# The selected-value pages of sample 7 are issued by SyncE in place of GpSimd

## The reference, cut to what matters

```
z = x @ w_in                                   # one projection for all groups
nsa_past = cache_nsa_kv[l, page_table]         # 8 samples x 16 pages of 128 rows, [cmp_k, cmp_v, sel_k, sel_v]
imp = einsum('bqn,ns->bqs', p.sum(axis=2), cover)     # importance of blocks of 64 rows
_, idx = top_k(imp, 16)                        # first block and two local ones always in
kg, vg = ks[bi, idx], vs[bi, idx]
sc = einsum('bqhd,bqjsd->bqhjs', q, kg) * ATTN_SCALE
o_sel = einsum('bqhjs,bqjsd->bqhd', softmax(sc), vg)
...
mix = concat([y_conv, o_nsa, o_moba, y_pool]) @ w_out
x = layer_norm(ALPHA * x + mix);  x = layer_norm(ALPHA * x + square(relu(x @ w_up)) @ w_down)
```

## Time and profile before

| | |
|---|---|
| Runs shown | 795.03, 796.51, 799.62 us |
| Median | 796.51 us |
| The profiled execution | 796.34 us |
| Its span | 794.6 us |
| Mean granted TensorE clock | 0.983 |
| Busy, share of the span | PE 95%, DVE 54%, ACT 35%, POOL 26% |
| selV pages by GpSimd (L1438) | 64 issues of 32 KB |
| selV pages by SyncE (L640) | 64 issues of 32 KB |

### The profile page before, as it was taken

One profiled execution on the slowest core, in us unless ns is written; L12 is line 12 of the kernel. 1 busy time (PEld: TensorE's weight loads), 2 busy tenths in 40 slices (PEclk: granted clock), 3 DMA queues, 4 the chain that ended last, 5 costly groups with the idle time before them and its releaser, 6 DMA issues.

```text
span 794.6 us, 17023 instructions
## 1 busy us (share of the span) xinstructions
PE 752.9 (95%) x6744; PEld 658.2 (83%) x6744; DVE 433.0 (54%) x744; ACT 281.8 (35%) x542; POOL 206.5 (26%) x268
## 2 busy tenths in 40 slices
PE   9999999988887999799999999999999999999992
PEld 8998988764554555369999999999999999999991
DVE  4878994554545543445866656534563255533535
ACT  5232234544535322342444454312431134311124
POOL 0000625012224555100837731000210012100083
PEclk9999999989999999899999999999999999999997
DMA  9656762547789885312252333332323322333102
GB/s 336 178 157 174 211 191 74 212 170 283 277 283 310 243 282 159 126 38 81 71 185 80 84 103 105 108 94 75 99 80 107 105 77 86 106 85 102 54 1 108
DMA packets 62680, 113.26 MB, mean 143 GB/s; under 512 B 16873, under 2 KB 34026, under 8 KB 61930
## 3 DMA queue, kind: packets, MB, share of 16 engines
q1 hardware_dynamic: 56074, 95.40, 38.7%
q0 software_dynamic: 6528, 16.78, 6.3%
HBM read 107.72 MB, written 6.52 MB: 144 GB/s over the span
## 4 chain that ended last, share of the span: by engine, by line
PE 75%; issue 8%; DVE 7%; DMA 3%; ACT 3%; POOLq 3%; POOL 1%; ACTq 0%; DVEq 0%
PE psum L723 58%; PE psum L732 4%; POOLq L1437 2%; DMA moba_lo<-in_moba_pages 1%; DMA moba_hi<-in_moba_pages 1%; PE psum L777 1%; PE psum L840 1%; PE psum L1004 1%; PE psum L808 1%; DVE yc L1579 1%; POOLq L1428 1%; DVE wL L1510 1%; PE psum L854 1%; PE psum L750 1%; PE psum L992 1%
## 5 line engine op out<-in xcount | busy, mean ns | idle before, releaser
L1510 DVE TENSOR_TENSOR wL<-raw,wH 128x1024 fp32r<-128x1024 f32 (+1 forms) x92 | 117.7, 1280 | 94.0 <-ACT wH L1155 94.0
L1155 ACT ACTIVATE wH<-raw 128x1024 fp32r<-128x1024 f32 (+1 forms) x92 | 94.0, 1022 | 120.4 <-PE psum L723 119.9
L723 PE MATMUL psum<-oxH,wH 128*128 128x260 f32 (+1 forms) x512 | 105.0, 286 | 1.5 <-DVE wL L1510 0.9
L723 PE MATMUL psum<-oxH,wL 128*128 128x260 f32 (+1 forms) x512 | 103.9, 284 | 0.0
L723 PE MATMUL psum<-oxL,wH 128*128 128x260 f32 (+1 forms) x512 | 103.4, 283 | 0.0
L723 PE MATMUL psum<-hidH,wL 128*128 128x260 f32 x512 | 103.2, 283 | 0.0
L723 PE MATMUL psum<-hidH,wH 128*128 128x260 f32 x512 | 103.2, 283 | 0.0
L723 PE MATMUL psum<-hidL,wH 128*128 128x260 f32 x512 | 103.0, 283 | 0.0
L1474 POOL TENSOR_TENSOR hsq<-relu 128x520 f32<-128x520 f32 x32 | 33.8, 1055 | 218.7 <-ACT relu L1336 218.7
L723 PE MATMUL psum<-opH,wH 128*128 128x260 f32 x400 | 85.4, 295 | 2.1 <-DVE wL L1510 1.4
L723 PEld LDWEIGHTS psum<-oxH,wH 128*128 128x128 f32 x512 | 79.5, 189 | 3.3 <-issue 2.5
(11 more groups left out here) (357 smaller groups left out, 1152.9 us busy)
## 6 DMA issues: line engine op xcount, KB each, us to landing
raw<-in_panels SPq DMA_DIRECT2D x88, 512.0 KB, 3.7
nsa_ring<-in_nsa_pages SPq DMA_DIRECT2D x128, 96.0 KB, 2.3
moba_hi<-in_moba_pages SPq DMA_DIRECT2D x36, 256.0 KB, 4.8
moba_lo<-in_moba_pages SPq DMA_DIRECT2D x36, 256.0 KB, 4.5
moba_lo<-in_moba_pages POOLq DMA_DIRECT2D x28, 256.0 KB, 5.1
moba_hi<-in_moba_pages POOLq DMA_DIRECT2D x28, 256.0 KB, 5.1
xres<-in_xT SPq DMA_DIRECT2D x8, 260.0 KB, 5.2
xres<-in_xT SPq DMA_DIRECT2D x1, 2080.0 KB, 9.1
```

The costliest lines, as they stand in the source:

```text
L723: last = mm(out[:, hf, 0:cols], w, x[:, k, hf * HALF:hf * HALF + cols], start=(t == 0 and j == 0), stop=(t == KT - 1 and j == 2))
L1155: fn(wtiles(wH, wH3, n).rearrange("p a b -> p (a b)")[:, cols], raw[:, n % NRAW, cols], ACT.Copy).then_inc(h_done, 1)
L1510: tt(wtiles(wL, wL3, n).rearrange("p a b -> p (a b)")[:, cols], raw[:, n % NRAW, cols], wtiles(wH, wH3, n).rearrange("p a b -> p (a b)")[: ...
```

## The change

A constant names the samples whose pages GpSimd brings. It holds 1, 3 and 5; sample 7 (steps `selv` 28 to 31, 16 issues) leaves GpSimd and goes to SyncE. The place of the steps in the list stays.

```diff
@@ -95,6 +95,7 @@
 MB1, PAIR_T = 10, 10.5
+SELV_POOL = (1, 3, 5)
 NCN = sum(c[0] != "moba" for c in COLS)
@@ -633,7 +634,7 @@
                     load_unit(2 * n + 4)
-                elif kind == "selv" and n // 4 % 2 == 0:
+                elif kind == "selv" and n // 4 not in SELV_POOL:
                     if n == 0:
                         sp_.wait_ge(mm_done, N_IN_PANELS)
@@ -1428,7 +1429,7 @@
-                if kind == "selv" and n // 4 % 2 == 1:
+                if kind == "selv" and n // 4 in SELV_POOL:
 
                     if n == 4:
                         pool.wait_ge(mm_done, N_IN_PANELS)
```

## The result

The changed kernel took 789.13 us, the median of 5 runs (787.14 to 791.72), against 796.3 us for the kernel before beside it (5 runs, 795.03 to 799.62). The ratio is 0.9896, 95% interval [0.9866, 0.9925]. The profiled execution took 788.66 us, with a span of 786.9; the one before had 796.34 and 794.6. Among all runs of this document two, both of the first kernel of experiment 2 (800.81 and 800.83 us), fell into a slower state of the chip with a lower mean clock, and the ratios leave them out.

A forecast was written before the change was run, and what follows sets the result against it. TensorE, waiting for sample 7's last selected-value page, issued late by GpSimd, was taken as the bound. Stall 5.25 plus clock 2.01 gave 7.3 us off 796.34: 789.0 us, range 787.0 to 793.0 (forecast case 787 to 790.5).

The forecast's parts named there:

- The place of the bound: TensorE's wait before spv of sample 7: a microsecond gained there reaches the end unless something else is late next.
- The stall: TensorE's wait before spv of sample 7 falls from 5.45 to 0.2 us: gain 5.25, bounds 0.95 and 5.45.
- The clock: TensorE's granted clock stays at 1.00 behind the wait, so four instructions there save 2.01 us.
- The landing: Sample 7's last page on SyncE lands 2.9 us after issue, at 320.2; bounds 319.1 and 324.5.
- What is late next: WB's transposes on TensorE need VectorE's copies: 3 us of slack lose only 1.0 us; xres load costs 0.
- B: Transport, not issue, decides when pages land: 796.3, no change; chance 0.06, shared with another no-change rival.
- A: SyncE keeps its slow issue pace, 0.71 to 0.74 us: 791.5 or 795.4 us; chance 0.12.
- C: SyncE's ring backs up, each issue taking 1.387 us: slower, 804.3 us; threshold 0.89 us per issue; chance 0.04.

The follow-up runs named there:

- experiment 2: Kernel before, but GpSimd reads four page numbers with one load: for selected values and MoBA units, 792.39 us; for selected values only, 788.75 us.
- filling products: Kernel before, with five products of zeros on TensorE while it waits for sample 7's pages; 795.5 against 796.94 us.
- experiments 5 and 6: 5: changed kernel with eight of sample 7's pages on GpSimd, 788.97, 787.76 us; 6: changed kernel plus GpSimd reading four numbers per load, 790.89, and changed kernel alone, 789.46.
- experiment 8: Changed kernel with SyncE's last eight pages of sample 7 moved behind its load of xres; 797.14 us, ratio 0.999.
- changed, beside the split: Changed kernel, nothing altered, measured beside the kernel with eight of sample 7's pages on either queue; 791.1 us.
- changed, id by id: Changed kernel, but SyncE reads each page number of sample 7 with its own load; 796.34 us, kernel before 797.64 us.
- eight more on GpSimd: Kernel before, with the last eight pages of sample 6 on GpSimd too; 803.95 us, ratio 1.0069.

## Why the prediction was right

The predicted time was 789.0 us, the measured median 789.13; the stage gave 7.16 us where the sum had 7.26. That closeness is in part luck: the same kernel took 789.46 and 791.1 us in the later measurements. (A slip that changes nothing: the range's lower end is worked out as 1.5 under 789.0, which is 787.5 and not 787.0.)

- **The place of the bound.** Right. The wait before spv of sample 7 fell from 5.45 to 0.43, and nothing between 321 and 344 gave the time back: TensorE was busy 17.63 of the 17.70 us from 326.0.
- **The stall.** Predicted 5.25 us, measured 5.02. The last issue was forecast at 317.3 and came at 317.3, but by two errors that cancelled. The interval was taken as 0.56 us because GpSimd would be silent; it was (317.3 - 306.9) / 16 = 0.65. And sample 6's last issue, taken from before as 308.3, came at 306.9. With the interval that was measured and the old start the sum would have had 318.7 and a wait of 1.6. Reading SyncE's group of eight as the nearest row was the weak step; it left out that a group of 16 meets one or two issues of 0.8 to 1.9 us.
- **The clock.** Predicted 2.01 us from four instructions, start to start. Measured twice: 7.16 - 5.02 = 2.14 in the changed kernel, 2.04 with the filling products and the wait left in place.
- **The landing.** Predicted 2.9, measured 2.74 for the last page; but the median of its sixteen was 1.9, and in the three later profiles of this path (experiments 5 and 6) the last page took 1.6 to 1.8. There later issues ate what the shorter landing gave: the last one came 0.8, 0.4 and 0.1 us after the start of the last MoBA product, where this profile's came 1.3 before it, and the waits were 1.40, 1.02 and 0.84. The xres load behind the pages cost nothing: issued at 318.61 (forecast 317.9), landed after 8.3 us, read at 349.73. What experiment 8 adds is that its order was worth something: ahead of the last eight pages it cost the whole gain.
- **What is late next.** WB's copies start at 330.16 on VectorE, their reader (L1033) at 333.51: 3.35 us of slack, against 3.36 before. I had expected 1.0 us of it to go; it stayed, since VectorE waited less for ScalarE (0.37 us before L1796, 1.89 before).
- **The rivals.** B (transport) fell with experiments 2 and 5. A, a slower pace of SyncE, came true in the pace of two later profiles: from the last page of sample 6 to the last of sample 7 they had (319.1 - 308.0) / 16 = 0.69 and (316.7 - 305.3) / 16 = 0.71 us an issue. Its price did not: the waits were 1.40 and 0.84 and not 2.6, since the last page landed in 1.6 and 1.8 us and not in 2.9, and the second began earlier. C (SyncE backed up) did not occur even with 128 issues on one queue (24 of them took 14.6 us, 0.61 each); its threshold of 0.89 us an issue was almost reached when each page had its own load (0.84), and there the gain vanished. The Trainium skill's rule that spreading DMAs over queues saves only issue time ("DMA: Bandwidth & Descriptors", rules for kernel authors) agrees with what was saved here: the wait went because the last page was issued 5.3 us earlier, while its landing stayed (2.82 and 2.74). The words "usually small" for that time, in the same page's section "Issuing engines are not separate DMA queues", don't hold for these 32 KB pages, of which 16 took 15.1 us to issue and the last under 3 to land.

## What to carry to other kernels

Where many small transfers are issued one by one with a page number of their own, count the issues ahead of the last one that somebody waits for, times the interval in that queue, before looking at bandwidth. Two cures took the whole wait away here, 24.6 us of stage against 32.35: eight of the sixteen issues moved to the other queue, and one load of page numbers for four issues. Moving all sixteen, the change of this document, left 0.4 to 1.4 us of waiting. Price a TensorE stall at its length plus what the lowered clock costs behind it; here that was 2 us on 5.

## What the runs showed of the hardware

**The price of the lowered clock isn't in proportion to the wait.** The stage without a wait takes 24.57 us, and spv starts 0.88 after the start of the last product; the wait is counted from the product's end, 0.18 later in effect. What is left of each stage after that and the wait (one profile each):

```
kernel                          stage   wait    left for the clock
changed, beside the split       26.15    1.40   0.00
changed, id by id               31.56    3.98   2.83
behind the xres load            32.77    5.37   2.65
before                          32.35    5.45   2.15
eight more on GpSimd            40.28   12.01   3.52
```

The shorter wait of 3.98 us cost more clock than the one of 5.45. The stretches of the id-by-id kernel show that the clock was 0.94 over the wait itself and low only when the work came back:

```profile
...
321.80:325.70 3.90, 0.00 (x0) 0.00 (x0) 1.01 (x2) 0.00 (x0) 0.00 (x0) 0.94 0.57 106
325.70:328.30 2.60, 2.56 (x49) 1.37 (x50) 0.00 (x0) 0.95 (x2) 0.00 (x0) 0.50 0.60 243
328.30:333.00 4.70, 4.70 (x21) 1.90 (x20) 3.94 (x24) 1.90 (x4) 0.00 (x0) 0.60 0.62 266
...
```

In the kernel before, 0.82 was the mean over the wait, and the last two pieces of the wait, cut finer, show that part of the low clock fell where TensorE stood anyway:

```profile
...
323.00:324.00 1.00, 0.00 (x0) 0.00 (x0) 0.00 (x0) 0.00 (x0) 0.12 (x1) 0.72 0.27 72
324.00:325.40 1.40, 0.00 (x0) 0.00 (x0) 0.00 (x0) 0.00 (x0) 0.00 (x0) 0.50 0.01 1
...
```

The column behind the clock is the busy share of the DMA engines: 0.01 while TensorE still waited for the last page, so they were not full.

**The MoBA stage ahead scatters.** The last MoBA product starts between 316.55 and 326.03 us in the profiles (the kernel with all pages on SyncE left out), though TensorE's work ahead of it is the same, with other waits for MoBA units each time, while the part behind the first output panel is 443.15 to 443.42 us in all of them. As far as the profiles go that is most of the scatter of the times, and the reason why the stage and not the whole time tells effects under 2 us apart.
